# Gated DeltaNet inverse on one Trainium2 core: 16x16 diagonal blocks by substitution on GpSimd, three TensorE levels in place of six

## The reference

```python
g = jnp.cumsum(g, axis=-1)
decay = jnp.exp(jnp.where(incl, g[..., :, None] - g[..., None, :], -jnp.inf))
k_beta = k * beta[..., None]
a_mat = einsum("bhnid,bhnjd->bhnij", k_beta, k) * jnp.where(strict, decay, 0.0)
rhs = jnp.concatenate([v * beta[..., None], k_beta * jnp.exp(g)[..., None]], axis=-1)
sol = lax.linalg.triangular_solve(eye + a_mat, rhs, left_side=True, lower=True, unit_diagonal=True)
...
v_new = u_c - w_c @ s
o = qd_c @ s + qk_c @ v_new
s = s * exp(gl_c) + kd_c.T @ v_new
```

## Time and profile before

| | us |
|---|---|
| three runs | 3093.09, 3091.65, 3097.91 |
| median | 3093.09 |
| profiled execution, span from first to last instruction | 3090.6 |

### The profile page before, as it was taken

One profiled execution on the slowest core, in us unless ns is written; L12 is line 12 of the kernel. 1 busy time (PEld: TensorE's weight loads), 2 busy tenths in 40 slices (PEclk: granted clock), 3 DMA queues, 4 the chain that ended last, 5 costly groups with the idle time before them and its releaser, 6 DMA issues. The chain is left out here.

```text
span 3090.6 us, 44354 instructions
## 1 busy us (share of the span) xinstructions
PE 2986.4 (97%) x17907; PEld 2444.4 (79%) x17907; DVE 1349.4 (44%) x1965; ACT 1151.8 (37%) x1941; POOL 1161.8 (38%) x765
## 2 busy tenths in 40 slices
PE   6999999999999969899999999999999999999998
PEld 5778787877888846788887887878888888888887
DVE  5233232322479859677665343322223232332323
ACT  4231413243145449567665122332333333333232
POOL 2222121212122240033111433456665766666764
PEclk9999999999999979999999999999999999999999
DMA  4533232333544366110112445423232324332331
GB/s 113 180 134 122 76 118 84 126 105 109 172 164 151 136 213 214 67 53 22 74 41 95 163 161 175 138 92 108 85 108 82 108 83 136 89 101 85 115 110 61
DMA packets 239595, 353.16 MB, mean 114 GB/s; under 512 B 32928, under 2 KB 186272, under 8 KB 239392
## 3 DMA queue, kind: packets, MB, share of 16 engines
q1 hardware_dynamic: 239392, 350.32, 34.8%
HBM read 263.71 MB, written 96.36 MB: 117 GB/s over the span
## 5 line engine op out<-in xcount | busy, mean ns | idle before, releaser
L2668 DVE TENSOR_TENSOR x_tm<-m_ps,x_tm 128x512 f32<-128x512 f32 x384 | 264.9, 691 | 744.2 <-PE m_ps L104 744.2
L102 PE MATMUL pj_acc<-u_hi,pj_w_hi 128*128 128x512 f32 x1464 | 576.2, 394 | 10.6 <-DVE u_lo L823 10.6
L104 PE MATMUL pj_acc<-u_hi,pj_w_lo 128*128 128x512 f32 x1464 | 571.6, 390 | 0.0
L103 PE MATMUL pj_acc<-u_lo,pj_w_hi 128*128 128x512 f32 x1464 | 571.1, 390 | 0.0
L551 POOL TENSOR_TENSOR pj_w_lo<-pj_w_raw,pj_w_hi 128x1024 fp32r<-128x1024 f32 x61 | 159.3, 2612 | 721.6 <-ACT pj_w_hi L600 721.6
L102 PEld LDWEIGHTS pj_acc<-u_hi,pj_w_hi 128*128 128x128 f32 x1464 | 275.7, 188 | 85.6 <-issue 18.2
L2550 POOL TENSOR_TENSOR m_lo<-gate,held 128x1024 fp32r<-128x1024 f32 x96 | 237.9, 2501 | 269.8 <-ACT held L2467 269.8
L104 PEld LDWEIGHTS pj_acc<-u_hi,pj_w_lo 128*128 128x128 f32 x1464 | 275.7, 188 | 58.1
L103 PEld LDWEIGHTS pj_acc<-u_lo,pj_w_hi 128*128 128x128 f32 x1464 | 276.0, 188 | 56.1
L102 PE MATMUL m_ps<-held 128*128 128x512 f32 x768 | 298.9, 389 | 2.4 <-DVEq L2649 2.4
L102 PE MATMUL m_ps<-held,m_h_hi 128*128 128x512 f32 x768 | 299.5, 390 | 0.0
(11 more groups left out here) (301 smaller groups left out, 5264.9 us busy)
## 6 DMA issues: line engine op xcount, KB each, us to landing
gate<-in_w_mlp_dram SPq DMA_DIRECT2D x48, 1024.0 KB, 5.4
gate<-in_w_mlp_dram SPq DMA_DIRECT2D x96, 512.0 KB, 3.6
proj<-pj_stage SPq DMA_DIRECT2D x61, 768.0 KB, 3.5
pj_w_raw<-in_w_in_dram SPq DMA_DIRECT2D x61, 512.0 KB, 5.1
gate<-proj SPq DMA_DIRECT2D x24, 768.0 KB, 4.4
mo_w_raw<-in_w_out_dram SPq DMA_DIRECT2D x48, 256.0 KB, 2.7
rpb_bias<-pj_shut SPq DMA_DIRECT2D x48, 192.0 KB, 3.0
rpb_bias<-rpb_near SPq DMA_DIRECT2D x24, 384.0 KB
```

The costliest lines, as they stand in the source:

```text
L102: pe.matmul(out, w_hi, x_hi, start=first, stop=False)
L103: pe.matmul(out, w_hi, x_lo, start=False, stop=False)
L104: return pe.matmul(out, w_lo, x_hi, start=False, stop=last)
L2668: dve.tensor_tensor(xt, ps2[:, q % 4], xt, ALU.add).then_inc(added, 1)
```

## The change

The first 16x16 of each diagonal are inverted by substitution on POOL, for all 24 matrices of a head at once; PE then does three levels, from 16 to 128. For head 0 this stands ahead of its inverse, for the others in the recurrence of the head before:

1. `scores` and `queries` replace `amat`; masks and exponentials are written straight into `am` and `qk2`. The strict masks of the next head wait for the last level's S of this one.
2. Step 2: `cut_blocks` copies the 32x32 diagonal blocks out of `am` (ACT for one direction, DVE's transpose for the other, four pieces each). Step 3: `widen` transposes them so that each block lies in one partition.
3. POOL: `solve`, 30 linked instructions (a copy, a memset, and 28 TensorTensor).
4. Step 7: `narrow`, two DVE transposes back; then `place` copies the blocks into `un` (DVE) and `tn` (ACT and POOL).
5. `flip`, `at`, `reset` and the join masks other than that of size 16 are gone. A itself is now the stationary operand of S, and `un` the moving one. S and U work on tiles that are cut in both directions: pairs of 64x64 at the first level, pairs of 32x32 at the second, one 64x64 at the third.
6. The product of q with its decay goes from DVE to POOL, early in the inverse. ACT's two wide exponentials for it move to units 0 and 2. The tanh of z and its gate move into recurrence steps 4 and 5. The inclusive exponentials of the next head move into the inverse.
7. The early loads of the merge stage that land in `am` wait for the last S in place of the output norm.

```diff
 
 HEADS = 4
-LEVELS = 7
...
@@ -1304,20 +1304,19 @@
         pool.memset(tile, 0.0).then_inc(chain, 1)
         keep(n + 1, tile, [[col, P]], base, row, fill)
...
-            pool.wait_ge(chain, n)
-            pool.memset(work[:], 0.0).then_inc(chain, 1)
-            pool.wait_ge(chain, n + 1)
-            pool.memset(blocks, 1.0).then_inc(chain, 1)
...
@@ -1326,25 +1325,30 @@
 BOTH = SEG[1][1] // P
...
-UNITS = LEVELS * 2 * NTB
-NS = UNITS - 2 * NTB
-NTR = NS - 2 * NTB
+NG6 = 2 * NTB
+ORDER = (0, 3, 4, 5, 1, 2)
+GRAMS = (2, 0, 1)
+PREP = (4, 5, 0, 1, 3, 2)
+NS = 3 * NG6
+NTR = 2 * NG6
 U_LAG, T_LAG = 2, 4
-UN_ORDER = (0, 3, 4, 5, 1, 2)
+Q32 = tuple(slice(32 * q, 32 * q + 32) for q in range(4))
...
+SQUARES_AT, ROOT_AT, EG_AT, CEXP_AT = 1, 5, (0, 2), 10
+LENGTHS_AT, MEAN_AT, DIAG_AT, SPREAD_AT, NORM_AT, GATE_AT = 2, 3, 5, (7, 9, 11), (8, 10, 12), 12
+TURN_AT = (0, 3, 6, 9, 11, 13)
+TOKEN_AT = ((1, 2), (4, 5), (7, 8), (10, 11), (12, 13), (14, 15))
...
+INCL_AT = {8: 4, 11: 5, 13: 0, 15: 1}
+STRICT_LAST = (4, 5, 0)
+STRICT_MID = {0: 1, 1: 2}
+STRICT_END = {0: 3}
+INCL_END = {1: 3, 3: 2}
+AMAT_IN = {0: (4, 5), 1: (0, 1), 2: (3, 2)}
+QK_IN = {0: (4, 5), 1: (0, 1), 4: (3, 2)}
+CUT_IN, WIDE_IN, ZTANH_IN, ZGATE_IN, SPREAD_IN = 2, 3, 4, 5, 7
+SOLVE = 2 + 2 * 14
...
-        diag = am[:, 0:NTB].rearrange("p a b n -> p (a b) n")
+        diag = four(work[:])
...
+        def parts(level, d):
+
+            if level == 0:
+                return [(r, r) for r in halves]
+            if level == 1:
+                return [(Q32[2 * h + d], Q32[2 * h + 1 - d]) for h in range(2)]
+            return [(halves[d], halves[1 - d])]
...
-            sp.wait_ge(S["onorm"], NTB * (HEADS - 1))
+            sp.wait_ge(S["s_mm"], NS * HEADS)
...
-            def reset(buf, n):
-                pool.tensor_copy(buf[:, n], ident[:].unsqueeze(1).to_broadcast([P, 4, P])).then_inc(S["u0"], 1)
...
+            def decayed_queries(i):
+
+                for d in range(2):
+                    pool.wait_ge(S["eg"], i * 2 + d + 1)
+                    if d == 0:
+                        pool.wait_ge(S[f"y_in{i % 2}"], i // 2 * 48 + 48)
+                    pool.tensor_tensor(gq[:, i % 2, d], gq[:, i % 2, d], y2[:, i % 2, 0], ALU.mult).then_inc(S["qd"], 1)
...
+            def solve(i):
+
+                c = Chain(pool, S["solve"], i, SOLVE)
+                both = [528, 2]
+                pool.wait_ge(S["wide"], i + 1)
+                if i:
+                    pool.wait_ge(S["spread"], 2 * i)
+                squares = [both, [32, 16], [1, 16]]
+                c.link(pool.tensor_copy(strided(sol, 0, squares), strided(c2, 0, squares)))
+                c.link(pool.memset(strided(sol, 0, [both, [33, 16]]), 1.0))
+                for j in range(1, 15):
+                    n = 15 - j
+                    term = strided(part, 0, [[j * n, 2], [n, j], [1, n]])
+                    right = strided(sol, j + 1, [both, [32, j], [1, n]])
+                    c.link(pool.tensor_tensor(term, strided(sol, j, [both, [32, j], [0, n]]),
+                                              strided(c2, 33 * j + 1, [both, [0, j], [1, n]]), ALU.mult))
+                    c.link(pool.tensor_tensor(right, right, term, ALU.add))
+                c.end()
...
+            def place(i):
+
+                pool.wait_ge(S["spread"], 2 * i + 1)
+                if i:
+                    pool.wait_ge(S["t_ev"], i * NTR)
+                    pool.wait_ge(S["u_mm"], i * NS)
+                for q in Q32:
+                    pool.tensor_copy(by_direction(tn, q, 1)[:, :, :, q], compact(c1, q, 1)).then_inc(S["tn0_pool"], 1)
...
+            for buf in (c1, sol):
+                pool.memset(flat(buf[:]), 0.0).then_inc(S["cleared"], 1)
+            for buf in (un, tn):
+                pool.memset(buf[:].rearrange("p a j n -> p (a j n)"), 0.0).then_inc(S["cleared"], 1)
...
+            solve(0)
+            place(0)
             for i in range(HEADS):
-                if i == 0:
...
+                decayed_queries(i)
...
+                    pool.wait_ge(S["o_mm"], i * 24)
+                for n in PREP:
+                    masked(qk2[:, (i + 1) % 2, n], i + 1, n, incl).then_inc(S["mask_i"], 1)
+                for k, n in enumerate(ORDER):
+                    pool.wait_ge(S["s_mm"], i * NS + 2 * NG6 + k + 1)
+                    masked(am[:, n], i + 1, n, strict).then_inc(S["mask_s"], 1)
+                solve(i + 1)
+                place(i + 1)
...
+                for q in Q32:
+                    act.copy(compact(c1, q, 0), by_direction(am, q, 0)[:, :, :, q]).then_inc(S["cut_a"], 1)
...
+                    for n in STRICT_LAST:
+                        strict_decays(i + 1, n)
...
+                        if step == CUT_IN:
+                            cut_blocks(i + 1)
+                    if step == ZTANH_IN:
+                        act.wait_ge(S["z_in"], i * 16 + 16)
+                        act.wait_ge(S["onorm"], NTB * i)
+                        act.activation(work[:], zt, ACT.Tanh, scale=0.5).then_inc(S["zt"], 1)
+                if more:
+                    place(i + 1)
...
+                        k, n = step, ORDER[step % NG6]
+                        if k < NG6:
+                            pe.wait_ge(S["un0"], i * 16 + (4, 8, 4, 8, 12, 16)[k])
...
                         for j in range(4):
-                            if k < SMALL:
-                                for r in halves:
-                                    last = pe.matmul(ps[r, k % 2, j, r], at[:, n, j, r], tn[:, n, j, r], start=True, stop=True,
-                                                     tile_position=(0, r.start))
-                            else:
-                                a, b = halves[1 - UN[n][1]], halves[UN[n][1]]
-                                last = pe.matmul(ps[a, k % 2, j, b], at[:, n, j, a], tn[:, n, j, b], start=True, stop=True,
-                                                 tile_position=(0, a.start))
+                            for x, y in parts(k // NG6, UN[n][1]):
+                                last = pe.matmul(ps[x, k % 2, j, y], am[y, n, j, x], un[y, n, j, y], start=True, stop=True,
+                                                 tile_position=(y.start, x.start))
...
                         for j in range(4):
...
+                            for x, y in parts(k // NG6, UN[n][1]):
+                                last = pe.matmul(ps[x, 5 + 2 * (k % 2), j, y], tn[x, n, j, x], sbuf_s[k % 4][x, j, y], start=True,
+                                                 stop=True, tile_position=(x.start, x.start))
...
-                        if i and 6 + k in OUT_AT["spread"]:
-                            out_spread(i - 1, OUT_AT["spread"].index(6 + k), 3)
+                        if i and k in SPREAD_AT:
+                            out_spread(i - 1, SPREAD_AT.index(k))
...
+                for q in Q32:
+                    dve.transpose(compact(c1, q, 1), by_direction(am, q, 1)[:, :, :, q]).then_inc(S["cut_d"], 1)
...
+                dve.transpose(c2[:], c1[:].rearrange("p m c -> p c m")).then_inc(S["wide"], 1)
...
+            def narrow(i):
+
+                dve.wait_ge(S["solve"], (i + 1) * SOLVE)
+                dve.wait_ge(S["wide"], i + 1)
+                dve.transpose(c1[:].rearrange("p m a -> p a m"), sol[:].rearrange("p b a -> p a b")).then_inc(S["spread"], 1)
+                dve.transpose(c2[:].rearrange("p m b -> p b m"), sol[:]).then_inc(S["spread"], 1)
+                dve.wait_ge(S["spread"], 2 * i + 2)
...
+                for d, src in ((0, c1), (1, c2)) if first else ((1, c2), (0, c1)):
+                    t = (slice(0, NTB, 2) if d == 0 else slice(1, NTB)) if first else slice(1 - d, 2 - d)
+                    for q in Q32:
+                        dve.tensor_copy(by_direction(un, q, d)[:, t, :, q], compact(src, q, d)[:, t]).then_inc(S["un0"], 1)
...
-                for v in range(LEVELS):
-                    for n in range(2 * NTB):
...
-                        dve.copy_predicated(un[:, n], join[:, v, d].unsqueeze(1).to_broadcast(wide),
-                                            at[:, n] if v == 0 else ps[:, bank]).then_inc(S["u_ev"], 1)
```

More of the change, by code:

```diff
@@ L42 @@
 HEADS = 4
-LEVELS = 7
+BASE = 16
 FF = 4096
@@ L1607, in main @@
                         act.copy(nb[:, j], ps[:, j, 1]).then_inc(S["new_ev"], 1)
-                    if more:
-                        for n, q in EXP_MID.get(step, ()):
-                            exponentials(i + 1, n, q)
+                    if more and step in STRICT_MID:
+                        strict_decays(i + 1, STRICT_MID[step])
                     for j, d, t in live_chains(step):
@@ L1763, in main @@
                                   start=True, stop=True).then_inc(S["new_mm"], 1)
-                    if more:
-                        prepare(i + 1, step)
+                    if more and step < 2:
+                        gram(i + 1, 1 + step)
                     for j, d, t in live:
@@ L1777, in main @@
```

(47 more changed lines are left out.)

372 lines of the change are left out of this document (164 added, 208 removed).

## The result

The changed kernel takes 3060.5 us (median of 4 runs, 3056.8 to 3062.2), the kernel before 3092.4 on the same chip: a ratio of 0.9888, 95% interval 0.9876 to 0.9900. It is faster, as forecast, by 32 us where the forecast had 67; the time lies 1.5 us inside the range's upper end of 3062.

The account below looks back on a forecast made before the run. PE's instruction stream was taken to set the pace of an inverse. The terms -30.1 - 84.3 + 20.6 + 18.6 + 8 = -67.2 took the median from 3093.1 to 3026 us; range 2988 to 3062.

Parts of the forecast that it names:

- clock at four restarts: PE's clock after its idle time before each head's inverse: 2 us lost at each of four restarts, +8.
- (b): Rival, first level of the inverse: diagonal tiles don't overlap, 8.6 us more a head, 3060 us; chance 0.12.
- (c): Rival: the clock stays low through the inverse's first level, some 6 us more a head, 3050 us or more; chance 0.08.
- (e): Rival: DVE or ACT becomes the bound of the inverse, each with about 25 us of work; 3035 to 3060; chance 0.1.
- Head 0's start: Before head 0's first S: nothing hides cut, widening, substitution, transposes and copies; +20.6 us.
- the lower bound: The substitution on POOL with 0.10 us fixed per instruction and no cost for runs: 10.4 us.
- the bound of twice the price: Head 0's start: DVE transposes at double the price of an elementwise operation of that size, +5.6 us.
- The inverse: 18 units in place of 36, paced by PE: -30.1 us in head 0, -28.1 in each of heads 1 to 3.
- this sign: Sign that the prediction is wrong: PE idle inside the inverse, put down to DVE or ACT; no size given.
- What costs nothing: In the inverse and before gram: POOL's product of q, its masks and the later loads add no time.
- (a): Rival: quick solve of 10.4 us, hidden between heads, and up to 13 us from cheap 32x32 tiles; 2982 to 2996; chance 0.2.
- Between heads: Recurrence to the next head's S: the substitution's chain ends at 44.6 us against 38.4; +6.2 a head, +18.6 for three.

Follow-up runs that it names:

- b1: On a1, the last two of six turns to token order, their token products and VectorE's gate moved to later units; 3030.8 us, ratio 0.9785.
- c1: On b4 with ScalarE's two exponentials two units later: unread TensorE products, 12 before head 0's first unit, 4 before that of heads 1 to 3; 3044.4 us.
- a3: On the changed kernel, unread TensorE products: 28 before head 0's first unit, 4 at its thirteenth, 5 before the first of heads 1 to 3; 3086.6 us.
- a4: The changed kernel without the last 7 of the substitution's 14 steps, so it doesn't compute the layer; 3049.2 us, ratio 0.9856.
- b3: On a1, VectorE's four cuts of a next head's blocks moved behind the state updates of the third recurrence step; 3048.9 us, ratio 0.9846.
- a1: The changed kernel with head 1's columns out of GpSimd's way and ScalarE's first inclusive exponential two units later; 3048.1 us, ratio 0.9848.
- d1: The changed kernel with four unread TensorE products put into the 3.6 us gap of head 0's inverse; 3056.1 us, ratio 0.9876.
- b4: The edits of a1, b1 and b3 together; 3030.7 us, ratio 0.9789.
- c4: On b4, one column sum of the last head's squares in place of twelve, so it doesn't compute the layer; 3028.4 us, ratio 0.9787.

## Why the prediction was right, and why by half

The sum against the traces, in us (gram to first unit; first unit to the next gram or, in head 3, to the second step; then to the next first unit):

| | before | forecast | changed | b1 |
|---|---|---|---|---|
| start of head 0 | 14.7 | 35.3 | 34.8 | 34.9 |
| inverse 0 | 62.1 | 32.0 | 42.7 | 32.4 |
| inverse 1 | 68.6 | 40.5 | 50.7 | 43.3 |
| inverse 2 | 70.1 | 42.0 | 52.0 | 45.3 |
| inverse 3 | 72.2 | 44.1 | 50.2 | 46.7 |
| between heads, three times | 38.4 | 44.6 | 46.8, 46.1, 46.2 | 46.4, 46.3, 46.7 |
| end of head 3 | 31.6 | 31.6 | 33.7 | 33.7 |
| clock at four restarts | | 8 | in the rows above | |
| sum | 434.5 | 367.3 | 403.0 | 375.7 |

The time is in the range by its end, and that is luck in good part: the forecast's own figure was 3026, the 0.45 that it had lay between 3005 and 3045, and the range was drawn out to 3062 for rivals (b), (c) and (e). Of these (b), whose 3060 is the measured time, is refuted below, and the other two hold in part.

**Head 0's start** was right as a sum (20.6 forecast, 20.1 measured) out of errors that cancel. The solve takes 12.6 us, not 16.4. POOL's groups in it:

```profile
L1542 POOL TENSOR_TENSOR dn_sol<-dn_sol,dn_part 128x28 f32<-128x28 f32 (+6 forms) x14 | 4.8, 345 | 1.1
L1540 POOL TENSOR_TENSOR dn_part<-dn_sol,dn_c 128x28 f32<-128x28 f32 (+6 forms) x14 | 4.7, 335 | 1.1
```

That is 9.5 us for 28 links of 0.23 to 0.42 us, and some 0.08 between them: runs cost nothing visible. (By its own terms the lower bound, 0.10 fixed and no runs, is 10.7 and not 10.4.) The transposes are dearer, 1.9 to 2.0 us each where 1.2 was put (the bound of twice the price was the nearer one), and narrowing and widening give back 2.2 of the 3.8.

**The inverse** is the term that failed: 10.7, 10.2, 10.0 and 6.1 us too little, 37 in all, of which the 8 for the clock were foreseen. The step that failed is that PE's instruction stream would still set the pace when it shrinks from 62 to 32 us, because DVE and ACT keep their total. Their total did fit (24.5 and 24.5 us of 42.7), their order did not: a table load with four exponentials, POOL's masks against DVE's columns, a gate behind a norm, each under 4 us, were hidden while a unit took PE 1.67 us, and are not when it takes 1.1. The prediction's last paragraph had named this sign, PE idle inside the inverse and put down to DVE or ACT. A clock that falls behind such a gap costs about as much again or more: 6.4 us behind head 0's gap of 3.6. The forecast had a clock term for the restarts only. b1 takes most of these waits away, and its inverses are 32.4, 43.3, 45.3 and 46.7, or 9.1 us in all above a forecast whose clock term was 8. That the sum closes so well is partly chance, for one price of the forecast was too high: S and U of a unit of the second level take 0.54 us at full clock (T to T is 1.11, less 0.57 to 0.59) and not 1.08, the half that the forecast had named and not taken. That is 3.2 us a head or 13 in all, so with the right price the forecast would have been 3013. By that estimate the waits and the clock cost the changed kernel's inverses about 42 us beyond the clock term, and not the 29 that the table gives.

**What costs nothing** named POOL's q product and masks as hidden. They were, for PE; for DVE they were not: 1.2 us in place of 0.17 for an operation of 12 columns.

**The rivals.** (c) has the mechanism but not its place: it put the low clock into the first level, where c1 and a3 show that it costs next to nothing in heads 1 to 3, and what it cost stood in the second half. (e) named DVE or ACT as the bound and gave 3035 to 3060, at whose upper end the time fell; they are it in stretches, not by their sum. (Its 25 us of work for each are 31 for DVE and 24 for ACT by the terms that it gives; 29.3 and 28.8 came, of head 1's 50.7.) (b) is refuted: 16 records of the first level's S and U, each a pair of 64x64 tiles on the diagonal and in one bank, take 0.51 us from start to start:

```profile
1289.48 0.68 PE L1758 MATMUL dn_ps<-dn_un,dn_am 64*64 64x64 f32 x16
1289.99 0.63 PE L1774 MATMUL dn_ps<-dn_ss,dn_tn 64*64 64x64 f32 x16
```

the same as the earlier trace rows. The rule cited with it from the Trainium skill ("TensorEngine Tiling (Array Packing)", Restrictions and Gotchas, Gotcha 1) shows no price here; the two tiles write different partitions. (a) had the quick solve half right (12.6 us, between its 10.4 and the forecast's 16.4) and the cheap 32x32 tiles wholly. What it gave the solve, 6 us at head 0 and 6.2 at each of the three others, a4 confirms for head 0 alone: between heads the solve is 1.1 us of the path.

**Between heads** 6.2 was forecast and 8.4, 7.7 and 7.8 came. PE idles 4.9 us ahead of S (7 forecast) and 2.0 at step 3. The slow clock of the inverse's end reaches into the first steps (0.50 until 1330.0): from gram to the second step it is 8.6 us where it was 6.3. Of the 35.8 us by which the stage took longer than forecast, 29.0 are the inverses beyond the clock term, 5.2 this, 2.1 the end of head 3 (a wait of 1.4 us for ACT's copies is in it; the rest wasn't followed), less 0.5 at the start.

Open stays why the clock falls behind one wait and not behind another of the same length (b3 and a1, c1's heads 1 and 2), and whether filling the gap would pay, since the run that filled it has no usable trace.

## What to carry to other kernels

When the busiest engine's work is cut in half, price the others by their longest piece between two of its units, not by their sum: what was hidden under units of 1.67 us stalls units of 1.1. Beside a stall in dense TensorE work, reckon with a half clock on the work behind it: 6.4 and 6.7 us here behind stalls of 3.6 and 5.8. Look in the windows for the clock behind a stall before explaining anything else; then leave a whole unit between the producer and the consumer (b1, 19 us) before trying idle products (a3 and c1, which cost time; d1 undecided). A chain moved off TensorE pays where something hides it: half of the solve is worth 6 us in head 0, and 1 or less in the others.

## What the hardware showed beyond this

A stretch in which PE is busy without a pause can lower the clock as a gap does: 24 records with one moving column (3.3 us) in a stretch at 0.62 of b4, 1.00 in c4 without them. It need not: in head 3 of b4 the clock stayed at 1.00, as it did before over the same records (2.7 us) and in head 1 of the changed kernel (2.8 us). A DVE transpose of 128x1024 in 32x32 blocks takes 1.9 to 2.0 us in fp32, 1.6 times an elementwise operation of that size (1225 ns in the earlier trace rows). POOL's small two-input operations go down to 0.23 us for 28 elements and 0.40 for 112.
